# A hybrid encoder step on one core: the constants' load moved, a gate block split, and waits interleaved with matmuls

## What is computed

```
z = x @ w_in            # columns: rnn stream | q | k | v | rnn gate | attn gate
A = RG-LRU(causal conv of width 4 over the rnn stream)       # linear recurrence per token
B = rotary GQA: 16 query heads, 2 key heads of 64; band of 3 chunks of 64, sinks;
    the sample tokens attend to 128 cached keys and their own 32
m = sigmoid(g_rnn) * (A @ w_br_rnn) + sigmoid(g_attn) * (B @ w_br_attn)
x = LayerNorm(alpha * x + m @ w_out)
scores = sigmoid(x @ w_router); 8 of 64 experts per token, from 4 of 8 groups
ff = (silu(x @ ws1) * (x @ ws3)) @ ws2                       # shared expert, hidden 256
   + sum over chosen experts of gate_e * (silu(x @ w1[e]) * (x @ w3[e])) @ w2[e]
x = LayerNorm(alpha * x + ff)
```

## Time and profile before

| | |
|---|---|
| median of the runs | 1609.67 us |
| the profiled execution | 1609.49 us, its span 1607.5 us, mean granted clock 0.996 |
| PE matmuls | busy 1569.8 us (98% of the span) |
| DVE, ACT | busy 742.2 us (46%), 569.4 us (35%) |
| DMA | 477.35 MB, mean 297 GB/s; about 400 GB/s in the expert stages |
| chain that ended last | PE 92%, DVE 4%, ACT 1%, DMA 1%, issue 1% |

### The profile page before, as it was taken

How to read it: one execution, slowest core, us unless ns; L and a number is a source line. 1 busy time by engine, 2 the same in 40 slices (tenths; PEclk the granted TensorE clock), 3 DMA queues, 4 the chain that set the end, 5 groups by cost and what they waited for, 6 DMA issues and landing times.

```text
span 1607.5 us, 25611 instructions
## 1 busy us (share of the span) xinstructions
PE 1569.8 (98%) x9496; PEld 1039.8 (65%) x9496; DVE 742.2 (46%) x1528; ACT 569.4 (35%) x1134; POOL 23.0 (1%) x38
## 2 busy tenths in 40 slices
PE   8999999999999999999999999999999999999997
PEld 7978997655454555555588789975555555554554
DVE  5658667333333423332474786662433332333336
ACT  4766434222232223222267564342223222222322
POOL 2000000000000000000010000000000000000000
PEclk9999999999999999999999999999999999999998
DMA  8553356499999999999536434458999999999991
GB/s 232 175 197 105 126 165 242 176 389 405 406 383 411 401 396 408 393 405 393 212 119 207 164 106 139 155 212 322 382 410 397 398 402 403 394 399 409 391 407 42
DMA packets 141588, 477.35 MB, mean 297 GB/s; under 512 B 10052, under 2 KB 74116, under 8 KB 108756
## 3 DMA queue, kind: packets, MB, share of 16 engines
q1 hardware_dynamic: 139760, 473.50, 76.4%
q0 software_dynamic: 1408, 2.85, 0.6%
q10 hardware_dynamic: 356, 0.13, 0.0%
HBM read 474.88 MB, written 1.57 MB: 296 GB/s over the span
## 4 chain that ended last, share of the span: by engine, by line
PE 92%; DVE 4%; ACT 1%; DMA 1%; issue 1%; SPq 0%; DVEq 0%; ACTq 0%
PE ps L943 27%; PE ps L963 14%; PE ps L582 6%; PE ps L583 6%; PE ps L584 6%; PE ps L569 5%; PE ps L984 4%; PE ps L925 4%; PE ps L985 4%; PE ps L926 4%; PE ps L928 2%; PE ps L972 1%; DMA dense<-in_w_in 1%; PE ps L905 1%; PE ps L951 1%; PE ps L725 1%
## 5 line engine op out<-in xcount | busy, mean ns | idle before, releaser
L943 PE MATMUL ps<-experts,xg 128*64 128x512 f32 x2048 | 450.5, 592 | 0.0
L943 PEld LDWEIGHTS ps<-experts,xg 128*64 128x64 f32 x2048 | 147.8, 137 | 290.6 <-issue 289.7
L963 PE MATMUL ps<-experts,hidT 128*64 128x512 f32 x1024 | 233.8, 598 | 1.0 <-ACT hidT L1309 1.0
L582 PE MATMUL ps<-parts 128*128 128x288 f32 x736 | 224.1, 304 | 4.0 <-DVE dense_lo L1438 3.7
L584 PE MATMUL ps<-parts,dense_lo 128*128 128x288 f32 x736 | 217.4, 295 | 0.0
L1765 DVE TENSOR_TENSOR hid<-ps,hid 128x256 f32<-128x256 f32 x64 | 27.2, 425 | 385.1 <-ACT hid L1303 385.1
L1317 ACT ACTIVATE yh<-ps,gsl 128x512 fp32r<-128x512 f32 x128 | 88.0, 687 | 230.0 <-PE ps L963 230.0
L1303 ACT ACTIVATE hid<-ps 128x256 f32<-128x256 f32 x64 | 24.5, 384 | 397.6 <-PE ps L943 397.6
L1295 ACT ACTIVATE xg<-ps,gperm_all 128x256 f32<-128x256 f32 x256 | 130.6, 561 | 63.6 <-PE ps L928 60.0
L1777 DVE SCALAR_TENSOR_TENSOR yl<-ps,gsl,yh 128x512 fp32r<-128x512 f32 x128 | 96.1, 751 | 122.7 <-ACT yh L1317 122.7
L963 PEld LDWEIGHTS ps<-experts,hidT 128*64 128x64 f32 x1024 | 68.2, 136 | 121.0 <-issue 121.0
(11 more groups left out here) (290 smaller groups left out, 2019.5 us busy)
## 6 DMA issues: line engine op xcount, KB each, us to landing
experts<-in_w SPq DMA_DIRECT2D x384, 1024.0 KB, 9.4
dense<-in_w_in SPq DMA_DIRECT2D x33, 1024.0 KB, 5.5
dense<-in_w_br_rnn SPq DMA_DIRECT2D x8, 1024.0 KB, 5.2
dense<-in_w_br_attn SPq DMA_DIRECT2D x8, 1024.0 KB, 5.2
dense<-in_w_out SPq DMA_DIRECT2D x8, 1024.0 KB, 5.2
dense<-in_ws SPq DMA_DIRECT2D x6, 1024.0 KB, 5.5
tok<-in_x_prompt SPq DMA_DIRECT2D x2, 512.0 KB, 4.5
dense<-in_w_in SPq DMA_DIRECT2D x2, 512.0 KB, 7.6
```

The lines of the kernel that those rows point to most:

```text
L582: mm(bank[:, 0:T], w_hi[:, k, col:col + P], hi[:, k, :], start=k == 0, stop=False)
L943: last = mm(ps[e % 2 * CAP:(e % 2 + 1) * CAP, 2, :], xg[:, k, e * CAP:e * CAP + CAP], experts[:, e, 0:2, k * DE:k * DE + DE], start=k == 0 ...
L963: last = mm(ps[e % 2 * CAP:(e % 2 + 1) * CAP, 3 + b, :], hidT[:, m, e % 2 * CAP:(e % 2 + 1) * CAP], experts[:, e, 2, m * D + b * 512:m * D ...
```

## The change

- SP issues the rest of the constants behind the third piece in place of the second.
- PE runs the first gate block in two halves: entries 0 to 3 of its 8 feature chunks ahead of the wait for the emptied gates, 4 to 7 behind the sample scores. The first two gate blocks wait for an older item (i - 4). ACT frees the first gate block ahead of the decay exponentials. DVE makes the product gx * u ahead of the copies of the key rows and the maxima.
- PE runs the first of the two blocks of the second shared matrix ahead of the ranks.
- PE runs seven of the eight blocks of the shared output ahead of the turn and the last behind it; it waits for both banks behind the next `up`.
- ACT normalises each full tile in two halves of 512 columns, with the next tile's root between them.

```diff
-                    if L == 0 and d == 1:
+                    if L == 0 and d == 2:
                         sp.dma_start(cst[:, P:NCONST], inp["consts"][:, P:NCONST]).then_inc(consts_in, 16)
...
+                elif i < Z_GATE + 2 and i >= Z_GATE:
+                    pe.wait_ge(z_free[i % 2], z_count(L, i - 4) + 1)
                 elif i >= Z_GATE:
                     pe.wait_ge(z_free[i % 2], z_count(L, i))
...
+                def first_gate(ks):
+                    if 0 in ks:
+                        piece(L, D_G)
+                        bank_of(L, Z_GATE)
+                    return over_features(ps[:, z_bank(Z_GATE), :], D_G, 0, xk, T, ks)
...
-                gate_chunks(GATES_AHEAD[0][:1])
+                first_gate(range(4))
                 for b in range(2):
                     pe.wait_ge(z_free[b], z_count(L, Z_GATE))
...
                 last.then_inc(s_scores, 1)
+                first_gate(range(4, KC)).then_inc(z_ready[Z_GATE % 2], 1)
                 gate_chunks(GATES_AHEAD[0][1:])
...
-                def shared_up(j):
-                    if j > 0:
+                def shared_up(j, ms=range(ME)):
+                    if j > 0 and 0 in ms:
                         piece(L, D_ROUTER + 1 + j)
-                    for m in range(ME):
+                    for m in ms:
                         ks = range(0 if j + m else 2, KC)
                         last = over_features(ps[:, 4 + 2 * j + m, :], D_ROUTER + 1 + j, m * P, xk, T, ks)
-                    last.then_inc(sh_ready, 1)
+                        if m == ME - 1:
+                            last.then_inc(sh_ready, 1)
 
                 shared_up(0)
+                shared_up(1, range(1))
...
                 last.then_inc(ranks, 1)
-                shared_up(1)
+                shared_up(1, range(1, ME))
...
-                def quad(n, first=False, last=False):
+                def quad(n, first=False, last=False, meanwhile=None):
                     if not first:
                         up(n, 0)
                         combine(n - 1, range(0, 4))
+                    if meanwhile:
+                        meanwhile(range(KC - 1))
                     turn(n, 0)
+                    if meanwhile:
+                        meanwhile(range(KC - 1, KC))
...
                     up(n, 1)
+                    if meanwhile:
+                        for b in range(2):
+                            pe.wait_ge(z_free[b], z_count(L, Z_SH2 + KC))
...
+                def half_rows(t, h):
+                    n = TOK[t][1]
+                    return activation(tok[0:n, t, 512 * h:512 * h + 512], ps[0:n, row_bank(k, t, h), :],
+                                      ACT.Identity, bias=mv[0:n, t, 0:1], scale=mv[0:n, t, 1:2])
+
                 root(0)
-                for t, (at, n) in enumerate(TOK):
+                for t in range(NT):
+                    act.wait_ge(norm_set, (2 * L + k) * NT + (t + 1))
                     if t < NT - 1:
+                        half_rows(t, 0)
                         root(t + 1)
-                    act.wait_ge(norm_set, (2 * L + k) * NT + (t + 1))
...
+                    half_rows(t, 1).then_inc(tok_act, 1)
...
+                act.wait_ge(xc_used, L + 1)
+                keep_gates(GATES_AHEAD[0][:1])
                 act.wait_ge(decay_set, 1)
                 for c in range(KC):
                     activation(a_[:, c, :], gl_[:, c, :], ACT.Exp, scale=c8[:, 0, L, c:c + 1]).then_inc(act_own, 1)
-                act.wait_ge(xc_used, L + 1)
-                keep_gates(GATES_AHEAD[0])
+                keep_gates(GATES_AHEAD[0][1:])
...
+                for b in range(2):
+                    dve.wait_ge(z_free[b], z_count(L, Z_GATE))
+                V.tensor_tensor(gxF, gxF, uF, ALU.mult).then_inc(gxu, 1)
                 dve.wait_ge(out_rows, 2 * L + 1)
                 V.tensor_copy(k_rows[:, 0, :], ps[:, 7, 0:P])
```

More of the change, by code:

```diff
@@ L894, in _, with shared_down @@
                 last.then_inc(ranks, 1)
-                shared_up(1)
-                def shared_down():
+                shared_up(1, range(1, ME))
+                def shared_down(cs):
                     d = D_ROUTER + 3
-                    piece(L, d)
-                    pe.wait_ge(sh_hid, (L + 1) * 2)
+                    if 0 in cs:
+                        piece(L, d)
+                        pe.wait_ge(sh_hid, (L + 1) * 2)
                     w = dense[:, d % RING, :].rearrange("p (m c) -> p m c", m=ME)
-                    for c in range(KC):
+                    for c in cs:
                         bank = bank_of(L, Z_SH2 + c)
@@ L906, in shared_down @@
                         last.then_inc(z_ready[c % 2], 1)
-                    for b in range(2):
-                        pe.wait_ge(z_free[b], z_count(L, Z_SH2 + KC))
                 def gather(n, added, js=range(4)):
@@ L1040, in round_of @@
                     up(q, 0, first=True)
-                    if meanwhile:
-                        meanwhile()
-                    quad(q, first=True)
+                    quad(q, first=True, meanwhile=meanwhile)
                     with pe.Fori(1, NQUAD - 1) as i:
@@ L1107, in root @@
                     activation(mv[0:n, t, 1:2], mv[0:n, t, 1:2], ACT.Sqrt).then_inc(dev_ready, 1)
+                def half_rows(t, h):
+                    n = TOK[t][1]
+                    return activation(tok[0:n, t, 512 * h:512 * h + 512], ps[0:n, row_bank(k, t, h), :],
+                                      ACT.Identity, bias=mv[0:n, t, 0:1], scale=mv[0:n, t, 1:2])
                 root(0)
-                for t, (at, n) in enumerate(TOK):
+                for t in range(NT):
+                    act.wait_ge(norm_set, (2 * L + k) * NT + (t + 1))
                     if t < NT - 1:
+                        half_rows(t, 0)
                         root(t + 1)
-                    act.wait_ge(norm_set, (2 * L + k) * NT + (t + 1))
-                    h = 0 if t < NT - 1 else 1
-                    activation(tok[0:n, t, 512 * h:D].rearrange("p (h c) -> p h c", c=512), ps[0:n, row_bank(k, t, h):row_bank(k, t, 1) + 1, :],
-                               ACT.Identity, bias=mv[0:n, t, 0:1], scale=mv[0:n, t, 1:2]).then_inc(tok_act, 1)
+                    half_rows(t, 1).then_inc(tok_act, 1)
             def norm_back(L, k):
@@ L1571, in _ @@
                 soften(0, sinkS[:, L, :, :].rearrange("p h a -> p (h a)"), n)
-                for b in range(2):
-                    dve.wait_ge(z_free[b], z_count(L, Z_GATE))
-                V.tensor_tensor(gxF, gxF, uF, ALU.mult).then_inc(gxu, 1)
                 normalise(0, [S[:, 0, h, a * 160:a * 160 + 160] for h in range(2) for a in range(2)], n)
```

## The result

The changed kernel takes 1596.67 us (median of 4 runs) against 1609.56: ratio 0.9922, 95% interval 0.9909 to 0.9934, so it is faster by some 13 us. The forecast was 1594.1, the range 1591.0 to 1599.5. Two things stand out: the single runs are 1595.25, 1595.49, 1597.85 and 1599.21, four microseconds apart where the kernel before kept within 0.4; and the profiled run, 1595.25, won 14.2 us against the 15.4 summed up.

What follows compares the result with a forecast made beforehand. PE was taken as the bound, busy nearly throughout, so edits win only what PE waits. Terms 5.2 + 2 x 3.1 + 2 x 0.2 + 2 x 1.7 + 0.2 = 15.4 us, from 1609.5 to 1594.1; range 1591.0 to 1599.5.

Steps and rivals of the forecast that it cites:

- the five terms: Gains summed over the changed places: 5.2 + 2 x 3.1 + 2 x 0.2 + 2 x 1.7 + 0.2 us.
- the three large ones: Start of layer 0, 5.2 us; sample scores, 3.1 us a layer; shared output round the turn, 1.7 us a layer.
- the second rival: Gather loses 0.5 us a layer and DVE's feature copies come 0.3 late at three norms: 1596.4; chance 0.12.
- Front: Start of layer 0: third weight piece ahead of the constants lands at 18.5, PE's seventh block starts at 31.6; 5.2 us won.
- the first rival: Start of layer 0: third weight piece lands late, at 22.6, beside `wax`; only 2.3 us won, 1597.0; chance 0.14.
- Sample scores: Both layers: gate block in halves, product ahead, decays behind the first gate; two short waits stay, 3.1 us a layer won.
- The role given to the product: Sample scores: DVE's product overran ACT's exponentials by 0.7 us; moved ahead, it sets DVE back 0.9, mostly covered.
- Ranks: Router, both layers: the 0.8 us selection wait goes but nearly all returns at the gather; 0.2 us a layer won.
- Shared output: Both layers: the eighth block behind the turn covers ACT's copy, first down matmul at 305.64; 1.7 us a layer won.
- Norm rows: Four norms, ACT rows in halves: second tile ready 0.2 us earlier at three, 0.35 lost at the last; together +0.2.
- two halves cost about 0.1 more: Norms: two ACT half rows take about 0.1 us more than the 1.19 us of one row of 1024.
- The fourth rival: PE's clock falls to half behind some 20 remaining gaps, 1.7 us each, 34 us in all: 1628; chance 0.02.

Runs made afterwards that it cites:

- the profiles of 1598.35 and 1597.81 us: Profiled runs of the changed kernel: repeated without edit (median 1597.68 us), and with POOL's `wax` loads held until the third weight piece landed (1597.81 to 1598.76).
- the last four experiments: Changed kernel with whole norm rows, each with one more edit: sample scores undone 1600.63, only gate halves kept 1594.52, shared output undone 1597.22, ranks undone 1594.93 us.
- the 1594.10 of an earlier set: Changed kernel with the norm rows undone (one ACT instruction of 1024 columns per tile): median 1594.10 us, ratio 0.9904 to the kernel before.

## Why the prediction was right, and where not

The time lay in the range because four of the five terms held, and the three large ones for the most part by the mechanism given. The median, 1596.67, is outside the forecast's own spread of 1592.0 to 1596.0; the range took it in because it was drawn to hold the rivals. That it stands 0.3 from the second rival's 1596.4 is chance: the gather did not lose, it gained 0.24 a layer.

**Front.** The third piece took the constants' rate (landing at 18.9, forecast 18.5; 18.5 to 19.1 in every profile with the constants behind it, so the first rival's 22.6 is out), the fifth block started without a gap, no half clock followed, and the seventh block came 0.3 later than the 31.6 of the forecast, because the small steps ahead of DVE's low half ended at 21.2, not at 20.8. The piece was through before most of `wax` moved: those four loads landed from 21.5 to 24.8. In the old order the piece ran from 17.7 to 24.9, right beside them (21.7 to 25.4). With `wax` held back it took no less, 3.3 us against 3.2. That 4.9 came so close to 5.2 is in part luck: both rest on the one profile before with its landing at 24.93, and two others in the old order have 23.82 and 22.98. The rule in the Trainium skill, "DMA: Bandwidth & Descriptors", section "Queues, rings and completion order", spoke for a late landing. Where small rows stand beside a load, the trace agrees with it: the constants, now behind the third piece and beside `wax`, took 3.8 us from 18.94 to 22.75, and 1.9 (18.61 to 20.47) when `wax` was held back; before, they took 2.3. The delay fell on a load that nothing waits for.

**Sample scores.** The third gate block starts 12.0 us behind the recurrence's end (12.1 forecast, 15.4 before). Two small waits were predicted and one came: 0.35 for the last query by the list, some 0.5 by starts, as the 0.6 of the forecast was counted; none for the normalised scores. The role given to the product was wrong: the halves remove the wait for the scores with the product in its old place as well.

**Ranks.** The wait came back at the gather in the two pieces named: 0.24 by the list, and 0.4 from start to start ahead of 279.31, where its neighbours stand 0.12 apart.

**Shared output.** 1.5 in place of 1.7: turn and down start as forecast to within 0.2 us.

**Norm rows.** The step that failed is "two halves cost about 0.1 more". ACT's halves at the first norm of the changed kernel, and DVE's first closing operation there and in the kernel before:

```profile
251.86 1.44 ACT L1126 ACTIVATE tok<-ps,mv 128x512 f32<-128x512 f32 x2
...
1583.67 1.20 DVE L1899 TENSOR_TENSOR tok<-tok,dense 128x1024 f32<-128x1024 f32 x1
...
1597.90 1.20 DVE L1880 TENSOR_TENSOR tok<-tok,dense 128x1024 f32<-128x1024 f32 x1
```

Halves back to back took 0.72 us each, so a row in halves ends 0.25 later than the 1.19 of the whole, and between the second tile's halves the next tile's root stands as well. The first half does start earlier, as said (PE's first gap 1.06 in place of 1.18), but the second tile comes later (0.69 in place of 0.46), and that one ends the fill. At the end DVE's closing operations start 2.07 us behind PE's last matmul, 1.52 before: 0.55 lost, 0.35 forecast. The Trainium skill, "ScalarE: Activation LUTs", section "What ACT_TABLE_LOAD costs", has a fixed part for each ACTIVATE and more for each pointer operand. By that rule a half takes more than half the time of a row, and this trace agrees: 0.72 us against 1.19.

**The clock.** The fourth rival was given 0.02 because one gap of 1.37 us had no fall behind it. That argument took gaps one at a time. Behind the fill's pair of 1.06 and 0.69, with 0.63 us of transposes between, the clock did fall, in the profiles of 1598.35 and 1597.81 us. Five of the changed kernel's nine runs lie 2.2 to 4.7 us above the other four, and one fall costs 3.1. The lower mean granted clock of each of the five says that the clock fell in all of them; where it fell is known of the one that has a profile. The runs show that the idle in this stretch is the cause: 1.07 + 0.69 falls in some runs, 2.04 + 0.47 lengthened all five, 1.18 + 0.46, 0.21 + 0.69 and 1.19 alone lengthened none of four runs each. The 18 runs of the last four experiments, which have 1.18 + 0.46 too, all kept 0.997 or 0.998. The sums are close (1.76 against 1.64 us); which property of the pair decides was not isolated. The Trainium skill, "TensorE: Matmul & The Clock Gate", section "A second HAM failure mode: psum-queue depth-cycling", has frequent short idles between matmul groups swing the clock. At this one pair the trace agrees; at the other places, gaps of up to 1.37 us before and 0.96 after passed at 1.00. The rival's mechanism was right at one place of each layer among some 20 gaps. By the granted clocks it accounts for the distance from the profiled 1595.25 to the median 1596.67, which lies midway between a short run and a long one; the norm rows, 1.0 lost where 0.2 was to be won, account for nearly all the rest of the miss.

What stays open: what decides, with equal gaps, whether a run falls. The run with `wax` held back reached the norm 0.39 us earlier and was long all five times, which may point to something in the timing ahead of the pair; no experiment varied that alone. Why the kernel before kept within 0.4 us in one set and spread over 4.5 in another was not examined either; the landing of its third piece, which differs by 2 us between profiles, and the fall in its front are candidates.

## What to carry to other kernels

Split a matmul block so that its first half needs only what is long free, and put the dependent step behind it: this gave some 3.0 of the 3.35 us a layer of the largest gain. Splitting an ACT row only pays when a consumer is signalled by the first half; without that signal it buys a later end. Look at gaps that follow each other as one place when the clock is at stake, and look at single runs with their granted clocks: a spread between runs of one kernel can be a cost of its own, and here one more pair of idle matmuls in the larger gap removed it. A gain read from one pair of profiles, like that of the front, wants a second pair.

## What was unexpected of the hardware

A matmul less can cost time: with one idle pair fewer ahead of a fill, all five runs were longer by 2.3 to 5.6 us than the 1594.10 of an earlier set, and with one more, the changed kernel's runs drew together to 1594.65 to 1594.86.
